# A row sum one slot behind the dot instead of three, on TensorE's queue of an expert layer woven into other stages

## The reference

```python
top_s, top_pos = lax.top_k(cand, PEER_TOPK)
experts = jnp.take_along_axis(cidx, top_pos, axis=-1)
gates = jax.nn.softmax(top_s, axis=-1)
...
def block(args):
    xb, eb, gb = args
    act = jax.nn.gelu(jnp.einsum('thkd,td->thk', u[eb], xb))
    return jnp.einsum('thk,thkd->td', (gb * act).astype(xb.dtype), v[eb])
```

## Time and the profile before

| | |
|---|---|
| median of three runs | 4357.79 us |
| the runs | 4362.82, 4357.79, 4352.83 us |
| time of the profiled execution | 4362.82 us |
| its span, first to last instruction | 4362.7 us |
| busy PE, DVE, ACT, POOL | 3036.8, 3040.3, 1425.9, 1605.5 us |
| mean granted TensorE clock | 0.843 |
| HBM traffic over the span | 350 GB/s |

### The profile page before, as it was taken

How to read it: one execution, slowest core, us unless ns; L and a number is a source line. 1 busy time by engine, 2 the same in 40 slices (tenths; PEclk the granted TensorE clock), 3 DMA queues, 4 the chain that set the end, 5 groups by cost and what they waited for, 6 DMA issues and landing times.

```text
span 4362.7 us, 34518 instructions
## 1 busy us (share of the span) xinstructions
PE 3036.8 (70%) x9655; PEld 1604.4 (37%) x9655; DVE 3040.3 (70%) x6138; ACT 1425.9 (33%) x4131; POOL 1605.5 (37%) x1308
## 2 busy tenths in 40 slices
PE   5699656865877744757768866767786787666665
PEld 1365342444433211423445333543354533222221
DVE  0406669867897847687757867868687688666766
ACT  1213322522233312235522332523463233232332
POOL 0001332423443424344423433334333354454553
PEclk8798777977999966878879988879888899888888
DMA  8143896888999999899979989999998999999998
GB/s 327 66 177 138 309 380 263 332 314 311 401 400 368 397 405 359 341 384 380 368 301 368 402 338 375 365 386 379 365 375 335 366 402 402 394 422 422 412 422 368
DMA packets 224712, 1529.11 MB, mean 350 GB/s; under 512 B 30877, under 2 KB 35169, under 8 KB 50710
## 3 DMA queue, kind: packets, MB, share of 16 engines
q0 software_dynamic: 186768, 1368.68, 78.5%
q1 hardware_dynamic: 37774, 158.45, 9.3%
HBM read 1523.79 MB, written 3.24 MB: 350 GB/s over the span
## 4 chain that ended last, share of the span: by engine, by line
DMA 32%; PE 29%; DVE 22%; issue 6%; POOL 4%; ACT 3%; SPq 1%; DVEq 1%; PEldq 1%; PEld 0%; ACTq 0%; POOLq 0%
DMA core_ring<-in_l_uv,core_experts 23%; PE sum_rows L1860 8%; DVE core_ring L1825 6%; DVE core_yv L1834 4%; POOL core_ring L1817 4%; PE sum_rows L2248 2%; PE j_in_ps L469 1%; PE j_query_pq L1613 1%; DMA s0a_query_w<-in_l_peer_wq 1%; PE s0b_query_pq L1613 1%; PE s0b_out_po L572 1%; DMA mod_w<-in_l_w_mod 1%; PE s1b_in_ps L469 1%; PE s1c_query_pq L1613 1%; DMA s1b_query_w<-in_l_peer_wq 1%
## 5 line engine op out<-in xcount | busy, mean ns | idle before, releaser
L1817 POOL DMA_INDIRECT core_ring<-in_l_uv,core_experts x1280 | 1592.4, 1244 | 2394.3 <-DVE core_yv L1834 1106.1
L1825 DVE CUSTOM_DVE_ANT_0 core_ring<-core_ring,core_hc 128x1024 f32<-128x1024 f32 x1280 | 1550.9, 1223 | 794.0 <-DMA core_ring<-in_l_uv,core_experts 465.9
L1860 PE MATMUL sum_rows<-core_ring,core_diag 128*128 128x512 f32 x3092 | 1664.0, 685 | 625.7 <-ACT core_diag L1852 526.5
L1860 PEld LDWEIGHTS sum_rows<-core_ring,core_diag 128*128 128x128 f32 x3092 | 629.1, 216 | 1585.3 <-ACT core_diag L1852 876.6
L1846 ACT ACTIVATE core_wt<-core_wt 128x1 f32<-128x1 f32 x1280 | 256.6, 200 | 1685.2 <-DVE core_wt L1825 1567.9
L1834 DVE SCALAR_TENSOR_TENSOR core_yv<-core_ring,core_wt,core_yv 128x1024 f32<-128x1024 f32 x507 | 649.4, 1281 | 10.8 <-ACT core_wt L1849 9.8
L1849 ACT ACTIVATE core_wt<-core_wt,core_gates 128x1 f32<-128x1 f32 x1280 | 376.8, 294 | 67.2
L1852 ACT ACTIVATE core_diag<-core_ident,core_wt 128x128 f32<-128x128 f32 x773 | 310.4, 402 | 25.2
L2248 PE MATMUL sum_rows<-core_ring 128*128 128x416 f32 x320 | 117.6, 527 | 5.2 <-DVEq L156 4.1
L1846 ACT ACT_TABLE_LOAD x81 | 103.9, 1283 | 5.2 <-DVEq L156 3.8
L1825 DVE DVE_READ_ACCUMULATOR2_ANT core_wt<- 128x1 f32 x1280 | 104.7, 82 | 0.0
(11 more groups left out here) (777 smaller groups left out, 3200.6 us busy)
## 6 DMA issues: line engine op xcount, KB each, us to landing
mod_w<-in_l_w_mod SPq DMA_DIRECT2D x16, 2048.0 KB, 12.3
core_ring<-in_l_uv,core_experts POOLq DMA_INDIRECT x1280, 11.0
core_ring<-in_l_w_mod POOLq DMA_DIRECT2D x8, 2048.0 KB, 10.3
p_in_w<-in_l_w_in SPq DMA_DIRECT2D x5, 1664.0 KB, 9.7
core_ring<-in_l_w_in POOLq DMA_DIRECT2D x5, 1664.0 KB, 8.8
p_query_w<-in_l_peer_wq SPq DMA_DIRECT2D x16, 512.0 KB, 4.4
s0a_query_w<-in_l_peer_wq SPq DMA_DIRECT2D x16, 512.0 KB, 9.0
s0b_query_w<-in_l_peer_wq SPq DMA_DIRECT2D x16, 512.0 KB, 8.2
```

The costliest lines, as they stand in the source:

```text
L1817: nc.gpsimd.indirect_dma_start(self.ring[:, r, :], None, core.a[f"l{layer}_uv"], bass.IndirectOffsetOnAxis(ap=self.experts[:, t, n:n + 1], ...
L1825: nc.vector.tensor_tensor_reduce(self.ring[:, r, 0:D], self.ring[:, r, 0:D], self.hc[:], 1.0, 0.0, ALU.mult, ALU.add, self.wt[:, r:r + 1]) ...
L1860: mm = nc.tensor.matmul(self.py[:, c * 512:(c + 1) * 512], self.diag[:, r, :], self.ring[:, r, D + c * 512:D + (c + 1) * 512], start=False ...
```

## The change

PE's lag in `upto` becomes one slot, except for the slots 0 to 3 of a tile, which keep three: DVE turns from one tile's running sum to the next (`turn_tile`) after the dot of slot 3, and PE's opening of the new sum stands at slot 0. The hardware loops, DVE's and ACT's orders, and the owners of the slots stay.

```diff
+    def lag(self, name, n):
+
+        return 1 if name == "tensor" and n % SLOTS > self.TURN_BEHIND else self.LAG[name]
+
     def upto(self, name, eng, goal):
 
         goal = min(goal, self.limit)
         self.own(goal)
-        while self.done[name] < goal - self.LAG[name]:
+        while self.done[name] < goal - self.lag(name, self.done[name]):
             self.step(name, eng, self.done[name])
             self.done[name] += 1
```

## The result

The changed kernel takes 4450.15 us (median; 4443.43 to 4452.68), the kernel before 4355.31 in the same comparison: a ratio of 1.0209, 95% interval 1.0186 to 1.0231, so 95 us slower. That is 50 us above the predicted 4400 and 4 above the upper end of the range. The profiled execution took 4452.68, its span is 4450.9, 88.2 more than before. The page's busy line answers to the earlier trace rows: the same instructions, PE busy 34 us longer, DVE the same.

The account below looks back on a forecast made before the run. No engine was full: the PE, ACT and DVE chain bounds s0b_gla, DMA the loops, late ring places attend. Losses of 87 less gains of 45 gave +42, 4400 us on the median, range 4355 to 4446.

Parts of the forecast that it names:

- +40, between 26 and 48: s0b_gla: PE's sums delay the next scores, 3.6 us over each of 10 even ticks, plus 3.7 at the stage's end.
- In the new order the sums come first and end no earlier than 820.30 + 3.70 = 824.00: s0b_gla, one even tick: two sums at 1.85 us each precede the next scores; the unit ends 3.3 us later.
- the clock: Second way to the dearer case (0.15 in all): waits slow later sums, +1.8 at some 14 blocked ticks, +25.
- three times 2.6, +8: s0a_gla: three even ticks, each with one newly weighed PE slot ahead of the scores; range 0 to 10.
- +28: Five first selects: PE sums two lead slots before its 32 score matmuls, DVE waits 5.7 us; range 17 to 31.
- +8 (5 to 11): Ends of three qk stages: PE's last transposes stand behind a newly waiting sum, 2.8 us each.
- 40 of 59: Attend stages: earlier release of ring places brings head-pair periods toward the loop's floor; gain 0 to 59, two thirds taken.
- no gain in attend: Dearer rival: ticks bunch requests, so attend transfers go no faster; +87 to +103, 4445 to 4461 us; dearer case 0.15.
- Nothing given back in the out stages: Out stages: no change, since all slots there are DVE's or weight loads end last.
- The "faster" rival: Attend reaches the loop's rate and GLA's waits vanish beneath DVE: -28, 4330 us on the median; chance 0.12.
- forecast of about 50 before that line: s0b_gla, profile after: DVE's idle before line 1164 rises from 14.6 to about 50 us.
- -5 for pool and tile ends: Tile ends come earlier and places are freed before each stage's barrier: -5 us, range 0 to -6.

Follow-up runs that it names:

- The experiment with zeros: Kernel before with one-slot lag only in the two GLA stages, plus 16 zero matmuls before PE's even ticks in s0b_gla and s0a_gla: 4405.18 us, ratio 1.0101.
- qk alone: Kernel before with the lag of one slot only in the three qk stages, three slots elsewhere: 4364.37 us, ratio 1.0016.
- GLA alone: Kernel before with the lag of one slot only in the two GLA stages, three slots elsewhere: 4418.8 us, ratio 1.0126.
- selects alone: Kernel before with the lag of one slot only in the select stages, entries included, three slots elsewhere: 4393.46 us, ratio 1.0081.
- their ticks alone: Kernel before with the lag of one slot only at select stages' ticks and end, three slots at their entries and elsewhere: 4345.11 us, ratio 0.998.

## Why the prediction failed

The direction was right, and so was the list of stages but for the out stages; sizes were not. Point by point:

- *s0b_gla, "+40, between 26 and 48".* Measured +58. The step that failed is "In the new order the sums come first and end no earlier than 820.30 + 3.70 = 824.00": it took the duration of the old order, in which PE idled 1.72 us ahead of them, for sums behind a wait of 4.74 to 5. There they took 5.34 to 6.78, so this term of the sum was too small by 2.4 us a tick. The prediction had the price of that, 3.68 us for a sum behind 3.43 us of idle, but put it into a rival ("the clock", +25) and not into the sum. The experiment with zeros shows the clock at 20 us and leaves 36 for the rest.
- *s0a_gla, "three times 2.6, +8".* Measured +16.6. The price came from s0b, where the unit of the earlier trace rows took 11.02 us. In s0a a unit was shorter. These are the scores(u,1) of two units before, and after:

```profile
475.74 0.94 PE L1029 MATMUL s0a_gla_pscore<-s0a_gla_qe,s0a_gla_e 64*128 64x128 f32 x12
...
484.96 0.94 PE L1029 MATMUL s0a_gla_pscore<-s0a_gla_qe,s0a_gla_e 64*128 64x128 f32 x12 [1.63 <-DVE s0a_gla_sc L1164]
```

```profile
487.58 0.94 PE L1029 MATMUL s0a_gla_pscore<-s0a_gla_qe,s0a_gla_e 64*128 64x128 f32 x12
...
493.68 3.78 PE L1860 MATMUL sum_rows<-core_ring,core_diag 128*128 128x512 f32 x4 [5.16 <-ACT core_diag L1852]
...
497.39 1.89 PE L1029 MATMUL s0a_gla_pscore<-s0a_gla_qe,s0a_gla_e 64*64 64x64 f32 x20
...
502.85 0.94 PE L1029 MATMUL s0a_gla_pscore<-s0a_gla_qe,s0a_gla_e 64*128 64x128 f32 x12
```

  9.2 us became 15.3: a chain set by ACT and PE has the same length in both stages, so the shorter stage loses more. The lower clock adds 1.9 us to the one sum here.
- *First selects, "+28".* Measured +28, by another route: the sums took 5.7 to 6.7 us instead of 3.7, and the scores behind them 3.73 instead of 6.69 in s1c.
- *qk, "+8 (5 to 11)".* Measured +15 (12.8 with qk alone). The last sum ahead of the transposes takes 3.78 us in s1a_qk and s1b_qk, at the lower clock (1.98 in p_qk), and waits ahead of such sums come several times in a stage.
- *Attend, "40 of 59".* Measured 51.5. The kernels here with the old order in attend took 536 to 545 us in these stages, those with the new one and places freed with the sum 492 to 495, so the gain is 41 to 53. The rival "no gain in attend" (4445 to 4461) holds the measured time, but only by chance, as attend did gain: DMA reached 390 to 405 GB/s there. The Trainium skill's 358 GB/s (page "DMA: Bandwidth & Descriptors", Specifications) isn't the limit of this single core; the measurement decides.
- *Nothing given back in the out stages.* This was missed. In s1b_out four matmuls (line 364) wait for a load from the modulation table. In the kernel before, two sums left over from attend ran beneath that load; after, PE stands 8.38 us. First before, then after:

```profile
2849.76 5.37 PE L1860 MATMUL sum_rows<-core_ring,core_diag 128*128 128x512 f32 x8 [2.07 <-DVEq L156]
...
2857.39 1.98 PE L364 MATMUL s1b_out_pt<-s1bq_room,core_ident 3*128 3x512 f32 x4 [1.40 <-DMA s1bq_room<-mods]
```

```profile
2950.28 3.78 PE L364 MATMUL s1b_out_pt<-s1bq_room,core_ident 3*128 3x512 f32 x4 [8.38 <-DMA s1bq_room<-mods]
```

  The load ends the wait in both kernels. The matmuls start 6.8 us behind its issue before and 8.7 after, and take 3.78 us instead of 1.98, the lower clock again. So s1b_out takes 5.4 us more. In all seven kernels with early sums in attend it takes 51.2 to 51.8 us, in the seven others 45.6 to 46.6; why the load lands later isn't shown. The 2.4 us of s1c_out can't be put down to attend: with the old order there it took 87.7 to 88.3 us in three kernels (GLA alone, selects alone, their ticks alone).

The "faster" rival fell at the point that was named for it: DVE's idle on the scores grew from 12.8 to 37.4 us at line 1164. The forecast of about 50 before that line was met by 39.0 there and 29.1 at line 1162, the first copy of every second unit, which it hadn't named. With the clock in the sum, 20 in s0b_gla alone, the forecast would have been about 4420, still below 4450; s0a, qk and the out stages make some 24 more, attend 11 less, 7 lie ahead of the first slot, and 10 are spread over other stages.

The prediction's -5 for pool and tile ends was met by -6 in the pool stages, which came with the change in GLA and not with the lag in pool: luck. Two slips in the prediction's sums change little: the upper bounds of the losses add to 104, not 103, and losses of 60 with gains of 55 give 4363 on the median, not 4370.

## What to carry to other kernels

Moving filler closer to its producer frees buffers earlier but puts a wait ahead of everything behind it in the same queue. So such a lag is a property of the stage, not of the kernel: short where the next real work waits for something later anyway (attend), long where the next work is ready (GLA, the entry of a select). When a price is taken from a trace, ask what the engine did just before: on PE the same sums cost 1.4 to 2 times as much here behind waits that the change itself creates.

## What the runs showed of the hardware

Matmuls of zeros onto an open sum kept the granted clock up: 0.93 instead of 0.82 over 220 us, and blocks of two sums back at 3.70 us. The Trainium skill, page "TensorE: Matmul & The Clock Gate", Part 1, says that an idle PE falls to half its clock; the rows agree (3.73 against 6.69 us for the same 32 matmuls). A fill that computes nothing paid here where PE would have idled anyway; in the kernel before, where scores stood ready behind it, the same fill cost 17 us in s0b_gla.
